# A hybrid decoder block on eight cores: the division of the attention moved out of the attention

## What is computed

```python
xn = rmsnorm(x, g_mix)
qa, ka, va, qr, kr, vr, gr, ga, gb = split(xn @ w_in)        # one projection, nine parts
# branch A: 16 heads of 64; three patterns (window, stride): (128,1), (512,4), (2048,16)
q, k = rotate(rmsnorm(qa)), rotate(rmsnorm(ka))
for each pattern: p = exp(q k / 8) under its mask;  num += p v;  den += sum(p)
y_att = (num / den) @ w_att                                  # the division in question
# branch B: retention, 4 heads, chunks of 128, decaying state 256 x 512, group norm, silu(gr)
y_ret = (rmsnorm(retention(qr, kr, vr)) * silu(gr)) @ w_ret
x = x + (sigmoid(ga + ba) * y_att + sigmoid(gb + bb) * y_ret) @ w_out
# then 32 experts, of which each token takes two
x = x + moe(rmsnorm(x, g_ffn))
```

## Time and profile before

| | us |
|---|---|
| median of three runs (lowest to highest) | 1601.79 (1600.74 to 1605.68) |
| the profiled execution | 1601.79 |
| its span on the slowest core, from the first to the last instruction | 1597.6 |
| spans of the eight cores | 1574.9 to 1597.6 |
| PE busy | 1370.9 (86%) |
| DVE busy | 763.3 (48%) |
| ACT busy | 695.2 (44%) |
| POOL busy | 762.8 (48%) |

### The profile page before, as it was taken

The page is one execution under the profiler, slowest core; times in us unless marked ns, Lnnn a source line. Parts: engine busy times, 40 slices in busy tenths (PEclk is TensorE's granted clock), DMA queues, the critical chain, the costliest instruction groups (busy, mean ns, idle before and its releaser), DMA issues.

```text
span 1597.6 us, 29878 instructions; the slowest of 8 cores (1574.9 to 1597.6 us)
## 1 busy us (share of the span) xinstructions
PE 1370.9 (86%) x10037; PEld 789.1 (49%) x10037; DVE 763.3 (48%) x1239; ACT 695.2 (44%) x1191; POOL 762.8 (48%) x874
## 2 busy tenths in 40 slices
PE   4899998888879999999999899999999736565675
PEld 2344547776744444444444444444445435454563
DVE  3787774766656556555656411111354652211122
ACT  3576668887853444434443411111233542222232
POOL 1379981333236657666756312221225645543453
PEclk9999999998999999999999999999999957887888
DMA  9747866786765769999994399875964785999985
GB/s 221 215 92 131 165 155 177 163 188 139 179 138 89 118 101 131 125 131 146 122 137 123 61 289 166 131 125 129 244 220 154 228 286 153 275 254 251 281 162 91
DMA packets 105502, 267.03 MB, mean 167 GB/s; under 512 B 43352, under 2 KB 65368, under 8 KB 98818
## 3 DMA queue, kind: packets, MB, share of 16 engines
q0 software_dynamic: 29280, 124.30, 49.7%
q1 hardware_dynamic: 76066, 140.76, 28.4%
HBM read 285.71 MB, written 116.65 MB: 252 GB/s over the span
## 4 chain that ended last, share of the span: by engine, by line
PE 69%; DMA 13%; DVE 5%; issue 4%; ACT 4%; POOL 2%; SPq 1%; another core or an unknown queue 0%; DVEq 0%; POOLq 0%; ACTq 0%
PE ps L169 69%; DMA arena<-xn,idx 8%; DMA zret<-arena 5%; DVE arena L169 4%; ACT arena L169 3%; POOL arena L169 2%; DMA cfs_sb<-cfs 1%; DVE arena L167 1%; SPq L169 1%; DMA vp<-arena 0%; DVEq L156 0%; DVE logit L169 0%; ACT L169 0%; POOLq L176 0%
## 5 line engine op out<-in xcount | busy, mean ns | idle before, releaser
L169 PE MATMUL ps<-arena 128*128 128x512 bf16 (+5 forms) x8208 | 1275.5, 313 | 78.5 <-ACT arena L169 32.5
L169 PEld LDWEIGHTS ps<-arena 128*128 128x128 bf16 (+1 forms) x8208 | 679.0, 102 | 587.1 <-issue 122.4
L169 ACT ACTIVATE arena<-ps 128x512 bf16<-128x512 f32 (+5 forms) x600 | 422.5, 719 | 450.6 <-PE ps L169 412.2
L169 POOL TENSOR_TENSOR arena<-arena 128x512 bf16<-128x512 f32 (+4 forms) x274 | 347.7, 1278 | 297.9 <-DVE arena L169 244.7
L169 DVE TENSOR_TENSOR arena<-ps,arena 128x512 f32<-128x512 f32 (+4 forms) x420 | 235.3, 572 | 347.0 <-ACT arena L169 159.8
L169 PE MATMUL ps<-cbs_sb,arena 128*128 128x128 bf16 x1408 | 131.1, 232 | 107.3 <-DMA arena<-xn,idx 69.7
L169 DVE SCALAR_TENSOR_TENSOR arena<-arena,ps 128x512 f32<-128x512 f32 x176 | 115.5, 683 | 192.3 <-PE ps L169 190.7
L169 PEld LDWEIGHTS ps<-cbs_sb,arena 128*128 128x128 bf16 x1408 | 100.7, 104 | 176.2 <-issue 147.8
L169 ACT ACTIVATE arena<-arena 128x8 f32<-128x8 f32 (+5 forms) x225 | 148.6, 665 | 59.0 <-DVE arena L169 29.1
L169 DVE TENSOR_TENSOR arena<-arena 128x1024 bf16<-128x1024 bf16 (+9 forms) x176 | 130.7, 750 | 75.7 <-ACT arena L169 68.7
L169 POOL DMA_INDIRECT out<-arena,idx x48 | 76.3, 1590 | 126.5 <-ACT arena L169 66.6
(11 more groups left out here) (60 smaller groups left out, 339.9 us busy)
## 6 DMA issues: line engine op xcount, KB each, us to landing
wb<-wexp POOLq DMA_DIRECT2D x60, 768.0 KB, 13.8
arena<-wb SPq DMA_DIRECT2D x30, 1536.0 KB, 15.4
arena<-x SPq DMA_DIRECT2D x32, 512.0 KB, 7.8
arena<-vx POOLq DMA_DIRECT2D x12, 768.0 KB, 5.1
arena<-wri POOLq DMA_DIRECT2D x8, 1024.0 KB, 23.1
zret<-arena SPq DMA_DIRECT2D x16, 512.0 KB, 19.8
arena<-zret SPq DMA_DIRECT2D x4, 2048.0 KB, 17.2
out<-arena SPq DMA_DIRECT2D x16, 512.0 KB, 9.8
```

The source lines that it names most:

```text
L169: ins = getattr(engobj, meth)(*a, **kw)
```

## The change

What is removed: the quotient beside the attention (`den_shift`, `den_act`, `z_out`, the two deferred calls), the tensor `zatt`, its four loads, and the mask by PE in two of four items per head.

What is put in: after a head, `head_out` stores the 64 numerator rows in float32 (512 KB) and one row of the denominators (8 KB) to DRAM. At the start of the retention all denominators come back as one tile `dall` of 128 x 256, DVE takes the reciprocal in one instruction, and it is stored as `rden`. From step 48 on, and in the merge, the quotients are made tile by tile (128 x 512): `div_load` loads 256 KB of numerators (`nb`) and twice 64 rows of 512 reciprocals, each a broadcast of one row of DRAM (`rb`); `div_mul` multiplies them on DVE into `za[c]`. In the words of the prediction a "set" is what one `div_load` brings. There are 32 sets, eight for each chunk `c`: those of chunks 0 and 1 in steps 48 to 61 with four buffers, those of chunks 2 and 3 in the merge with three.

```diff
 convert:
-  p.dma(wb_d[e][:, cs].rearrange("p (a b) -> p a b", a=2), wexp_d[e][:, cs].rearrange("p (a b) -> p a b", a=2),
+  p.dma(wb_d[e][:, cs].rearrange("p (a b) -> p a b", a=6), wexp_d[e][:, cs].rearrange("p (a b) -> p a b", a=6),
 load_wm:
-  load_cast(d[:, 0:2048], wm_d[fc][:, 0:2048], 1, Rwm[i][0], ("wm", i, 0))
-  load_cast(d[:, 2048:5120], wm_d[fc][:, 2048:5120], 2, Rwm[i][1], ("wm", i, 1))
+  load_cast(d[:, 0:2048], wm_d[fc][:, 0:2048], 4, Rwm[i][0], ("wm", i, 0))
+  load_cast(d[:, 2048:5120], wm_d[fc][:, 2048:5120], 6, Rwm[i][1], ("wm", i, 1))
 attention:
-        def den_shift(pr, e, hf): ...
-        def den_act(pr, hf, func, scale): ...
-        def z_out(pr, hf): ...
+        def head_out(pr, e):
+            h, r0, d0, i = 2 * pr + e, e * 64, 64 - e * 64, (2 * pr + e) % NXO
+            p.dma(num_d[h * 64:(h + 1) * 64, :], xo[i][r0:r0 + 64, :], reads=Rxo[i], writes=[Rnum[h]], semkey=("zatt", i))
+            p.dma(den_d[h:h + 1, :], xo[i][d0:d0 + 1, :], reads=Rxo[i], writes=[Rdend[h]], semkey=("xin", i))
...
-            queue.append((pr, eh, n_, S_item(pr, eh, kind, j, n_ in (2, 3, 4, 5))))
+            queue.append((pr, eh, n_, S_item(pr, eh, kind, j, n_ in (3, 5))))
 retention and merge, new functions:
+        p.dma(dall, den_d.rearrange("h (a b) -> (h a) b", a=8), reads=Rdend, writes=[Rdall], semkey="rawtab")
+        def den_rec():
+            OP("dve", "reciprocal", out=dall, in_=dall, reads=[Rdall], writes=[Rdall])
+            p.dma(rden_d.rearrange("h (a b) -> (h a) b", a=8), dall, reads=[Rdall], writes=[Rrden], semkey="gqkb")
+        def div_load(c):
+            pr, i = dv[0] % 8, dv[0] % len(nb)
+            dv[0] += 1
+            cs = slice(c * 512, c * 512 + 512)
+            p.dma(nb[i], num_d[pr * 128:(pr + 1) * 128, cs], reads=Rnum[2 * pr:2 * pr + 2], writes=[Rnb[i]], semkey=("vp", i))
+            for e in range(2):
+                p.dma(rb[i][e * 64:(e + 1) * 64, :], rden_d[2 * pr + e, cs].partition_broadcast(64), reads=[Rrden], writes=[Rrb[i][e]],
+                      semkey=(("zero", i // 2, i % 2), ("qz", i // 2, i % 2, False))[e])
+        def div_mul(c):
+            pr, i = dv[1] % 8, dv[1] % len(nb)
+            dv[1] += 1
+            OP("dve", "tensor_tensor", out=za[c][:, pr, :], in0=nb[i], in1=rb[i], op=ALU.mult, reads=[Rnb[i]] + Rrb[i],
+               writes=[Rza[c][pr]])
 retention, at the end of step s_:
-                if deferred:
-                    deferred.pop(0)()
+                if s_ == 1:
+                    den_rec()
+                if s_ == 48:
+                    za_alloc(0, 168)
+                    za_alloc(1, 192)
+                    div_bufs((176, 180, 184, 188))
+                    for u_ in range(4):
+                        div_load(0)
+                if 51 <= s_ < 62:
+                    for _ in range(1 + (s_ % 2 == 1 and s_ < 60)):
+                        div_mul(dv[1] // 8)
+                        if dv[0] < 16:
+                            div_load(dv[0] // 8)
-                if s_ == 57:
-                    areset(168 * KB)
-                    z_alloc(0)
-                    load_za(0)
+                if s_ == 62:
+                    zr_alloc(0, 176)
                     load_zr(0)
 between retention and merge:
-        for c in (1, 2):
-            z_alloc(c)
-            load_za(c)
-            load_zr(c)
+        zr_alloc(1, 64)
+        load_zr(1)
+        div_bufs((56, 60, 124))
+        for u_ in range(3):
+            div_load(2)
+        za_alloc(2, 80)
+        zr_alloc(2, 88)
+        load_zr(2)
+        za_alloc(3, 152)
 merge, after piece n of unit un:
+                pi = 5 * un + n
+                if pi >= 4 and dv[1] < 16 and (pi % 2 == 0 if dv[1] < 8 else pi % 3 == 0):
+                    div_mul(2 + dv[1] // 8)
+                    if dv[0] < 16:
+                        div_load(2 + dv[0] // 8)
```

More of the change, by code:

```diff
@@ L319, in build_nc @@
     wb_d = nc.dram_tensor("wb", [NE, 128, 6144], BF16, kind="Internal").ap()
-    zatt_d = nc.dram_tensor("zatt", [D, S], BF16, kind=skind).ap()
+    num_d = nc.dram_tensor("num", [D, S], F32, kind="Internal").ap()
+    den_d = nc.dram_tensor("den", [16, S], F32, kind="Internal").ap()
+    rden_d = nc.dram_tensor("rden", [16, S], F32, kind="Internal").ap()
     zret_d = nc.dram_tensor("zret", [2 * D, S], BF16, kind=skind).ap()
@@ L763, in build_nc @@
         xo = [alloc([128, S], F32, Rxo[i]) for i in range(NXO)]
[L764 to L767, removed]
+        Rnum = [p.res(f"num{h}") for h in range(16)]
+        Rdend = [p.res(f"dend{h}") for h in range(16)]
         slot = [0]
@@ L975, in build_nc @@
             g += 1
-        deferred = []
         for g in sorted(todo):
@@ L1021, in build_nc, with div_bufs @@
         assert apos[0] <= 167 * KB, apos[0]
+        areset(92 * KB, 96 * KB)
+        Rdall = p.res("dall")
+        dall = alloc([128, 256], F32, [Rdall])
+        Rrden = p.res("rden")
+        p.dma(dall, den_d.rearrange("h (a b) -> (h a) b", a=8), reads=Rdend, writes=[Rdall], semkey="rawtab")
+        Rnb = [p.res(f"nb{i}") for i in range(4)]
+        Rrb = [[p.res(f"rb{i}_{e}") for e in range(2)] for i in range(4)]
+        nb, rb, dv = [], [], [0, 0]
+        def den_rec():
+            OP("dve", "reciprocal", out=dall, in_=dall, reads=[Rdall], writes=[Rdall])
+            p.dma(rden_d.rearrange("h (a b) -> (h a) b", a=8), dall, reads=[Rdall], writes=[Rrden], semkey="gqkb")
+        def div_bufs(at):
+            assert dv[0] == dv[1]
+            del nb[:], rb[:]
+            for i, k in enumerate(at):
+                areset(k * KB)
+                nb.append(alloc([128, 512], F32, [Rnb[i]]))
+                rb.append(alloc([128, 512], F32, Rrb[i]))
+            dv[:] = [0, 0]
+        def div_load(c):
[11 more added lines that the diff above has]
+               writes=[Rza[c][pr]])
         INNER = ps[:, 3, 0:128]
@@ L1143, in build_nc @@
         za, zr = {}, {}
-        Rza = [[p.res(f"za{c}")] for c in range(NG)]
+        Rza = [[p.res(f"za{c}_{k}") for k in range(8)] for c in range(NG)]
         Rzr = [[p.res(f"zr{c}")] for c in range(NG)]
@@ L1210, in build_nc @@
         RmT = [[p.res(f"mT{c}_{k}") for k in range(8)] for c in range(NG)]
[L1211 removed]
+        mT = [alloc([128, 8, 512], BF16, RmT[c]) for c in range(NG - 1)]
+        areset(160 * KB)
         Rwo = [p.res(f"wo{i}") for i in range(2)]
         wo = [alloc([128, 8, 512], BF16, [Rwo[0]])]
[L1214 removed]
+        areset(116 * KB, 124 * KB)
         wo.append(alloc([128, 8, 512], BF16, [Rwo[1]]))
```

43 lines of the change are left out of this document (11 added, 32 removed).

## The result

The changed kernel takes 1645.89 us (median of 4 runs), against 1601.79 for the kernel before on the same chip (median of 3): a ratio of 1.0264, 95% interval 1.0234 to 1.0293. Ratios and times here compare only runs in the chip's faster state; in its slower one, as in a fourth run of the kernel before (1689.60 us), some cores show a lower granted clock and take longer. The forecast was 1579, the range ended at 1598. The slower side won, by none of the four rivals.

A forecast was written before the change was run, and what follows sets the result against it. PE was taken to bound retention and merge, with PE and nearly ACT full in the attention, where the quotient lengthened pairs. Attention -36, retention 0, merge +13 sum to -23 from 1601.79 us: 1579 us, range 1557 to 1598.

The forecast's parts named there:

- four rivals: Sets in time (0.30), half the attention (0.09), not what set the pair (0.05), small casts are slow (0.06).
- Quotient and masks, -36: Attention: quotient taken out and two masks per head moved to DVE together save 36 us, ends 26 and 43.
- pair of 21.7: Attention: a pair of heads was to take about 21.7 us after the change.
- the paragraph on stores: Attention: larger head stores and sooner Q and V loads both at nothing, as PE waits for no load.
- Half the attention: Rival: attention becomes bound by DMA or DVE's masks, gains 18, merge stop stays: 1597; chance 0.09.
- The masks' own 10.1 us: Attention: moving two masks per head from PE to DVE gains 10.1 us over 16 heads.
- First 16 sets in the late retention: Retention from step 48: first set or two slow, others in time; 0 us, bounds +13 and -4.
- sets in time: Rival: same attention gain, no stop in the merge, -2 in the retention: 1564; chance 0.30.
- Sets in the merge: Merge: chunk 2 ready 11 us or more after PE wants it at piece 22; +13, bounds 0 and +20.
- Small casts: Retention: casts cut into smaller pieces, counted within a term taken as 0.
- the rival of 1699: Rival: small cast pieces are slow, converts at twice the time start the merge 133 us late: 1699; chance 0.06.
- the rule weighed against the change: Trainium skill: transfers under 2 KB have a large cost of their own; 4 or 8 KB can be much faster.

The follow-up runs named there:

- e4: Kernel before with only two masks per head moved from PE to DVE: ratio 0.9989, attention 223.0 us.
- e1: Changed kernel with each reciprocal load taking 64 different rows of 2 KB instead of one row 64 times: ratio 1.0073.
- e12: Changed kernel with reciprocals loaded only once per buffer, so sets bring numerators alone: merge 304.4 us.
- e6: Changed kernel with the merge visiting chunk 2 ten pieces later and its products spaced out, same loads: ratio 1.0206, merge 328.8 us.
- e15: Changed kernel with reciprocals loaded once per buffer and the merge's later places for chunk 2 and the products: merge 297.7 us.
- e2: Changed kernel with the casts cut into pieces as in the kernel before: ratio 1.0283.
- e9: Kernel before with two masks per head on DVE and the quotient on POOL (power -1 and products): 4158.29 us.

## Why the prediction was wrong, point by point

*Quotient and masks, -36: the engines' part was right, its size on this chip was not.* A head became 10.61 us, near the 10.9 of my pair of 21.7, and with little DMA beside it the stage is 38 us shorter, near the 36 I gave. What failed is the paragraph on stores, which put the DMA beside the faster stage at nothing. I weighed loads that PE might wait for; what came late were PE's own instructions. Thinning the DMA around them gave back 16.0 us (196.4 to 180.4), 10.4 of them in waits for "issue". The list from which I took the earlier trace rows had that wait in its third row, 6.7 us, and I passed it over. "Half the attention" had named DMA and a gain of 18, at a chance of 0.09. The masks' own 10.1 us were wrong where a quotient stands beside them (e4: +4.4); without the quotient they were not tried apart.

*First 16 sets in the late retention, 0 with a bound of +13: the step that failed is the price of a piece.* I priced a set's 256 pieces at the rates of plain stores, 2 us outside the casts, and used that in the sum, in the bound and in "sets in time". I did not price a load that reads one row many times apart. The one in the trace of before would not have warned me: it brings a row of 8 KB 128 times, and from 452.8 to 459.2, alone on the queues but for one packet of instructions, it took 0.504 x 6.4 x 16 / 128 = 0.40 us per 8 KB, no more than eight pieces of 1 KB in the earlier trace rows.

```profile
q1 hardware_dynamic: 144, 1.05, 50.4%
arena<-g_ret_norm SPq DMA_DIRECT2D x1, 1024.0 KB, 6.3
```

The sets' 2 KB of one row, 64 times, took twice as long per packet, for numerators and reciprocals together; e1 puts that at 11.4 of the 20.4 us. Whether the length of the row makes the difference was not tried. The other 9 us are inside the bound, which was for such a case: a set in the stretch that the casts fill (e12).

*Sets in the merge, +13 with bounds 0 and +20: the same price, and a second error.* With different rows the merge loses 20.7 us (e1), the end of my range, and its stop in front of chunk 2 is 14.64 us long: the sum of bytes behind SP's list was sound for plain loads. One row added 26.8. The second error is one of place: I let the sets cost only where PE first needs chunk 2, at the 23rd piece. The first product stands at the fifth piece in DVE's list, with the accumulations of chunks 0 and 1 behind it. Later places gave 6.3 us with the loads of the change (e6) and 6.7 where no row is read many times (e12 to e15).

*Small casts, 0, and the rival of 1699: right to leave out.* e2 shows no effect, and the rule weighed against the change did not come true for casts. The number of packets is the same for either cut.

*The chances.* Both terms for the sets hung on one unseen price, so they failed together; a range of 1557 to 1598 and 0.06 for slower treated them as settled. The rival that won was none of mine: the casts' pieces were suspected, the broadcast's were not.

## What to carry to other kernels

A load that reads one source row many times can be another operation than a plain load of the same bytes and pieces: look whether the profile has one of the same piece length before pricing it, and if not, let the range reach to where it decides. When a wait is small, ask what it would be once the waits around it are gone. Work moved from an engine to a queue is paid by all that stands behind it in order: the engine's own list, the queue's other transfers, and the instructions that come by the same DMA engines. When a stage is relieved of its engines, ask whether its DMA share leaves room before counting the gain.

## What the hardware showed that was not expected

- One DRAM row of 2 KB read 64 times, with as many plain pieces: 0.211 us per packet in a stretch where 64 different rows took 0.107. The 2 KB packets alone: 0.264 and 0.125, and 0.349 with one SBUF partition read 64 times. A row of 8 KB read 128 times took 0.40 us per 8 KB, as plain pieces did.
- With sources of [2, 64, 512] the loads of sets kept 2.2 of 16 DMA engines busy, with [8, 8, 512] 8.1.
- A 16 KB packet of instructions stayed 2.1 us on its engine beside casts, and PE lost 16.2 us of 192 in waits for "issue", whose longer stops all end just after such a packet.
- A cast DMA cut into pieces a third or a quarter as long makes the same 29280 packets.
- POOL's power on 128x1024 float32 took 163 us, its product on 64x1024 2.3 (e9).
- After 27 us without work PE's clock stood at its lower level for the first 3 us of work.
